# Recurrent stage of a hybrid block: products with rows by direction, the second direction's time reversed, and full-row transpositions

## The chip, the cores and the metric

The kernel runs on one core of a Trainium2 chip. The metric is the device time of one execution in microseconds, as the median over runs. The core's engines are PE (matmul), DVE (VectorE), ACT (ScalarE), POOL (GpSimd) and SP (SyncE), each with its own program; they order each other by semaphores.

## The reference

Two transformer blocks on 512 tokens of 1024 features. The change lies in the second block's RWKV-7 mixer: four pairs of heads (head size 64), a forward and a backward scan over 256 context tokens (no output), then over 512 latent tokens from the state reached, and the two directions' outputs are summed. Cut to its core:

```python
def rwkv_scan(s0, r, decay, k, v, kk, a, reverse, emit):
    def step(s, inp):
        w_t, k_t, v_t, kk_t, a_t = inp[:5]
        s_kk = jnp.einsum('bhvk,bhk->bhv', s, kk_t)
        s = (s * w_t[:, :, None, :]
             - s_kk[..., None] * (kk_t * a_t)[:, :, None, :]
             + v_t[..., None] * k_t[:, :, None, :])
        y = jnp.einsum('bhvk,bhk->bhv', s, inp[5]) if emit else None
        return s, y
```

`decay` and `a` come, for each direction, from a low-rank product with its own bias (w0, w_lora_b, a0, a_lora_b); `kk` is the normalized key.

## The kernel before

The recurrent stage computes the scan in 12 chunks of 64 tokens, both directions in the same chunk: chunks 0 to 3 are the context (quiet: no output), chunks 4 to 11 the latent tokens (they emit). Everything is f32. A chunk has 16 matrices of 64x64: 4 head pairs (q) x 2 heads of a pair (h) x 2 directions (d). In SBUF a tile of 128 partitions x 64 columns holds the two heads of (q, d), one in each half of the partitions; eight such tiles (n = 4d + q) make an operand of 512 columns. A product is 16 matmuls of 64 rows, written by `tiles` (L2026, matmul at L2031): ALONG leaves a matrix on its half of the partitions, ACROSS changes halves. An operand with features on the partitions (kap, rho, kt, bt, state) is "feature-major", one with tokens there (AT, CT, R1, R2, vt, kT, bT, Gs, Us) "token-major".

For each chunk c:

- The decays, two chunks ahead. `lora_in_act` (L1918) makes the low-rank input (tanh, L1925), `lora_pe` (L2057) multiplies it: 16 matmuls with 64 rows and 128 stationary columns (L2068). DVE adds the bias (`logits`, L2285), ACT takes the sigmoid (L1934), DVE's scan sums over time (L2295, and L2297 with time reversed for direction 1), ACT exponentiates (L1941, L1942, L1944), and POOL and DVE multiply: kap (L1906), rho (L1909, emitting chunks), kt (L1914), bt (L2314).
- The pair products of chunk n = c+1, in banks of PSUM: AT = bt x kap, CT = kt x kap, R1 = kt x rho, R2 = bt x rho, and the transpositions kT, bT and vt as products with the identity. DVE masks CT, R1 and R2 out of PSUM (`masked`, L2334); ACT copies AT, kT, bT, vt (`pair_copy`, L1964). `pair_XT` and `pair_X` (L2330) prepare X = I + masked AT and its transpose.
- The inverse of the triangular matrix, in five levels l. `level_Y` (L2110): 16 matmuls of 32 columns; DVE's `level_y` multiplies them by the level's mask (L2345); `level_W` (L2121): 16 matmuls more; DVE's `level_x` adds (L2353) and transposes (L2357). Each of these is in two groups, by direction.
- The state products of chunk s = c-1: Gold = kap x state and Gnew = CT x vt into the same bank, copied by ACT (Gs); U = X^T x Gs, copied (Us); Z = kT x vt + bT x Us, added to the state by DVE (`state_add`, L2363) and decayed (`state_decay`, L2369); y, an old part rho x state and a new part R1 x vt + R2 x Us, copied by ACT for chunks 4 to 7 (`y_copy`, L1954) and added by DVE for chunks 8 to 11 (`y_sum`, L2376).

The order is written out by hand in the loops over c of `rwkv_pe`, `rwkv_dve`, `rwkv_act` and `rwkv_pool`. `beside` issues two products alternately, one tile of each in turn, `alone` one. Before, PE's order in a chunk is: Y1 beside Gold(s); Gnew(s); low-rank product of c+2; W1 beside vt(c); Y2; U(s); W2 beside AT(n); Y3 beside CT(n); W3 beside Z(s); Y4 beside kT(n); W4, first group, beside the old part of y(s); new part of y(s); W4, second group, beside bT(n); Y5 beside R1(n); W5 beside R2(n).

## Time and profile before

| | us |
|---|---|
| median of 3 runs | 3107.16 (3104.86 to 3117.13) |
| profiled execution | 3118.53 |
| its span | 3116.9 |
| recurrent stage, chunks 0 to 11 in the profiled execution | 2153.0 to 2448.3 |
| mean granted clock of TensorE, as a share of full speed | 0.950 |

Times in the trace are microseconds from the start of the span. A matmul in f32 leaves two records on PE and two weight loads on PEld, a transposition one of each. PEclk is the clock that was granted, as a share of the full 2.4 GHz. In a wait, "issue" means that the engine waited for nothing that the profile shows. A chunk is cut here where the first matmul of its level 1 starts.

### The profile page before, as it was taken

Reading aid. Unit: us, or ns where it says so; the run is one execution under the profiler, and the core shown is the slowest. Engines: PE = TensorE matmul, PEld = TensorE weight load, DVE = VectorE, ACT = ScalarE, POOL = GpSimd, SP = SyncE. Lnnn points to the kernel's source line nnn. Section 1 sums busy time; section 2 is a strip of 40 time slices with the busy share of each in tenths; the row PEclk is TensorE's granted clock in tenths of the full one; section 3 lists DMA queues with packets and bytes.
Section 4 is the critical chain, followed back from the end, with each engine's and each line's share of the span. In section 5 each row is a group of like instructions: output and inputs, shape, how many; then the busy total and the mean of one; then the engine's idle time right before and its main releaser. Section 6 shows DMA issues by size and latency. Waiting matters only on the chain. (4 is left out here: it accounts for less than half of the span.)

```text
span 3116.9 us, 53002 instructions
## 1 busy us (share of the span) xinstructions
PE 2816.6 (90%) x20916; PEld 2297.6 (74%) x20916; DVE 1773.3 (57%) x2734; ACT 1417.7 (45%) x1913; POOL 850.6 (27%) x515
## 2 busy tenths in 40 slices
PE   9999999998989899999997999997877688799996
PEld 7887877776768687788774787776777465688884
DVE  3115456788999642311445402446776554699996
ACT  4445545555663232444344222334433222588884
POOL 3444451220004343344432234222332131000001
PEclk9999999999999999999998999997998788899997
DMA  3225371112222132222552122221000023899996
GB/s 125 94 95 188 135 280 64 42 61 66 80 81 98 61 122 88 88 94 95 187 189 85 54 75 85 75 78 52 5 4 4 29 81 115 326 412 411 412 411 243
DMA packets 110379, 412.30 MB, mean 132 GB/s; under 512 B 12064, under 2 KB 12080, under 8 KB 109312
## 3 DMA queue, kind: packets, MB, share of 16 engines
q1 hardware_dynamic: 88560, 322.24, 28.4%
q0 software_dynamic: 11136, 48.26, 4.2%
q10 hardware_dynamic: 10512, 39.33, 3.5%
q8 instruction: 131, 2.15, 0.3%
q14 instruction: 40, 0.33, 0.0%
HBM read 370.45 MB, written 39.32 MB: 131 GB/s over the span
## 5 line engine op out<-in xcount | busy, mean ns | idle before, releaser
L219 POOL TENSOR_TENSOR ring_r<-ring,whi 128x1024 fp32r<-128x1024 f32 x241 | 591.3, 2463 | 1017.4 <-ACT whi L214 1008.0
L231 PE MATMUL psum<-xn_r,whi 128*128 128x512 f32 x1176 | 460.1, 391 | 0.0
L214 ACT ACTIVATE whi<-ring 128x1024 fp32r<-128x1024 f32 x247 | 256.0, 1054 | 421.1 <-DMA ring<-stream 420.8
L229 PE MATMUL psum<-xh,ring_r 128*128 128x512 f32 x936 | 388.6, 415 | 28.1 <-DVE ring_r L219 20.5
L2813 DVE TENSOR_TENSOR er_r<-er,eh 128x1024 fp32r<-128x1024 f32 x268 | 309.5, 1219 | 1.0 <-ACT eh L2802 0.4
L2802 ACT ACTIVATE eh<-er 128x1024 fp32r<-128x1024 f32 x268 | 268.2, 1072 | 40.3 <-DMA er<-experts 39.6
L2031 PE MATMUL psum<-mem 64*64 64x64 f32 (+1 forms) x7744 | 214.8, 231 | 69.8 <-issue 24.8
L229 PE MATMUL psum<-ffn_xh,ring_r 128*128 128x512 f32 x672 | 261.4, 389 | 0.0
L230 PE MATMUL psum<-ffn_xh,whi 128*128 128x512 f32 x672 | 261.4, 389 | 0.0
L2031 PEld LDWEIGHTS psum<-mem 64*64 64x64 f32 x7744 | 200.8, 145 | 81.2 <-issue 55.1
L231 PEld LDWEIGHTS psum<-xn_r,whi 128*128 128x128 f32 x1176 | 222.1, 189 | 47.3
L229 PEld LDWEIGHTS psum<-xh,ring_r 128*128 128x128 f32 x936 | 178.4, 191 | 85.4 <-DVE ring_r L219 24.1
L563 DVE TENSOR_TENSOR gu<-gu,psum 128x512 f32<-128x512 f32 x44 | 30.3, 688 | 335.0 <-ACT gu L538 335.0
L230 PE MATMUL psum<-xh,whi 128*128 128x512 f32 x504 | 198.8, 394 | 0.0
L467 DVE TENSOR_TENSOR mem<-mem 128x1024 f32<-128x1024 f32 x64 | 127.9, 2026 | 76.3 <-ACT mem L449 71.6
L231 PE MATMUL psum<-xn_r,whi_h 128*128 128x512 f32 x432 | 170.2, 394 | 0.0
L230 PE MATMUL psum<-xh,whi_h 128*128 128x512 f32 x432 | 170.2, 394 | 0.0
L229 PE MATMUL psum<-hid_hi,ring_r 128*128 (+1 forms) x352 | 144.6, 411 | 13.1 <-POOL ring_r L219 13.1
L2873 PE MATMUL psum<-er_r,xbh 128*128 128x512 f32 x368 | 146.7, 399 | 3.4 <-DVE er_r L2813 2.0
L229 PEld LDWEIGHTS psum<-ffn_xh,ring_r 128*128 128x128 f32 x672 | 126.1, 188 | 26.3
L230 PEld LDWEIGHTS psum<-ffn_xh,whi 128*128 128x128 f32 x672 | 126.1, 188 | 26.1
L2875 PE MATMUL psum<-eh,xbl 128*128 128x512 f32 x368 | 144.5, 393 | 0.0
(527 smaller groups left out, 6031.3 us busy)
## 6 DMA issues: line engine op xcount, KB each, us to landing
ring<-stream SPq DMA_DIRECT2D x311, 512.0 KB, 3.3
er<-experts SPq DMA_DIRECT2D x276, 512.0 KB, 8.2
mem<-mod_w ACTq DMA_DIRECT2D x48, 512.0 KB, 3.5
xs_dram<-zero_row POOLq DMA_DIRECT2D x1, 12288.0 KB, 41.6
xs<-xs_dram SPq DMA_DIRECT2D x23, 512.0 KB, 8.1
ys_dram<-y_t ACTq DMA_DIRECT2D x23, 512.0 KB, 6.7
spill<-resid POOLq DMA_DIRECT2D x2, 2048.0 KB, 26.6
resid<-spill POOLq DMA_DIRECT2D x2, 2048.0 KB, 9.9
```

What stands on the lines that cost most here:

```text
L214: act.activation(high_of(part, j), w, ACT.Copy).then_inc(w_hi, 1)
L219: pool.tensor_tensor(ring_r[:, s, :, :], ring[:, s, :, :], f(high_of(part, j)), ALU.subtract).then_inc(w_lo, 1)
L229: pe.matmul(bank, lo[:, b, :], x_hi_, start=start, stop=False, skip_group_check=True)
L230: pe.matmul(bank, hi[:, b, :], x_hi_, start=False, stop=False, skip_group_check=True)
L231: return pe.matmul(bank, hi[:, b, :], x_lo_, start=False, stop=stop, skip_group_check=True)
L467: dve.tensor_tensor(mod_t[at % 2], mod_wb[m % 4], mod_c[:, s, :], ALU.mult).then_inc(mod_mul, 1)
L563: dve.tensor_tensor(gu[:, half, :], gu[:, half, :], psum[:, 2 * half, :], ALU.mult).then_inc(sg_ready, 1)
L2031: ins = pe.matmul(psum[o, bank, first:first + wide], lhs(n)[r], rhs(n)[r], start=i == 0 if start is None else start, stop=i == len(terms) ...
L2802: act.activation(eh[:, SLOT[kind] + j, :], er[:, SLOT[kind] + j, :], ACT.Copy).then_inc(e_hi, 1)
L2813: dve.tensor_tensor(er_r[:, at, :], er[:, at, :], f(eh[:, at, :]), ALU.subtract).then_inc(e_lo_dve, 1)
L2873: pe.matmul(bank, x_hi_, lo_[:, cols], start=start, stop=False, skip_group_check=True)
L2875: return pe.matmul(bank, x_lo_, hi_[:, cols], start=False, stop=stop, skip_group_check=True)
```

## The change

- Rows go by direction. Token-major operands hold direction 0 on partitions 0 to 63 and direction 1 on 64 to 127, so the two groups of a level are now the heads of a pair (h), not the directions. The second direction is stored with its time reversed from the start (`seq` and rho's product read it with a step of -1), so one mask serves both directions (576 columns fewer are transferred) and DVE's scan runs one way.
- kap and rho lie side by side, and `joint` multiplies one stationary tile of bt by both: AT and R2 come from one product, 16 matmuls with 128 moving columns (64 in quiet chunks). Likewise CT and R1 from kt.
- kT, bT and vt are 12 full transpositions of 128x128 in a chunk (`turned`, L2104), no longer 48 matmuls of 64x64. For vt POOL first copies v into `vs` (two copies a chunk).
- The low-rank product is 8 matmuls of 128 rows over a block-diagonal input (`lwd`, filled by four activations in place of two), not 16 of 64.
- Gnew lies beside Y1 and Gold is alone; the state and y products go to other quadrants and banks (6 and 7).
- PE's order in a chunk is: Y1 beside Gnew(s); Gold(s); low-rank product of c+2; W1; Y2; U(s); W2 beside AT+R2(n); Y3; W3 beside Z(s); Y4; kT(n); bT(n); W4, first group, beside the old part of y(s); new part of y(s); W4, second group; Y5; W5 beside CT+R1(n); vT(n).
- ACT's copy of vt stands at the end of the chunk, before the second half of the decays of c+2 and the low-rank inputs of c+3.

The operands:

```diff
-        kap, rho = [take(W8, "b") for _ in range(3)], [take(W8, "b") for _ in range(3)]
-        bt, kt = take(W8, "b"), take(W8, "b")
+        turn = lambda v, d: v.rearrange("p (q d t) -> p q d t", q=4, d=2)[:, :, d, :]
+        KR = [take(2 * W8, "b") for _ in range(3)]
+        kap, rho = [v[:, 0:W8] for v in KR], [v[:, W8:2 * W8] for v in KR]
+        bt, kt, vs = take(W8, "b"), take(W8, "b"), take(W8, "b")
...
-        lw_c = take(2 * L, "b")
+        lwd = take(4 * L, "b").rearrange("p (m t) -> p m t", m=2)
...
-        M_BANK = dict(vt=6, AT=4, CT=6, kT=4, bT=5, R1=6, R2=4)
+        TURNED_BANK = dict(kT=2, bT=3, vt=2)
...
+            pool.memset(lwd, 0.0).then_inc(filled, 1)
...
+                    pool.tensor_tensor(turn(kap[c % 3], d), seq(None, c, d), half(pexc, d), ALU.mult).then_inc(pool_p.sem, 1)
...
-                        pool.tensor_tensor(half(rho[c % 3], d), seq(0, c, d), half(pinc, d), ALU.mult).then_inc(pool_p.sem, 1)
+                        o = first_token(c, d)
+                        decay = half(pinc, d)[:, :, ::-1] if d else half(pinc, d)
+                        pool.tensor_tensor(turn(rho[c % 3], d), Z[:, 0:4, o:o + L], decay, ALU.mult).then_inc(pool_p.sem, 1)
...
-                        pool.wait_ge(pe_m.sem, pe_m.at(c - 1, "R1" if emits(c - 1) else "kT"))
-                    pool.tensor_tensor(half(kt, d), half(tk, d), half(pinv, d), ALU.mult).then_inc(pool_p.sem, 1)
+                        pool.wait_ge(pe_m.sem, pe_m.at(c - 1, "CT"))
+                    pool.tensor_tensor(turn(kt, d), half(tk, d), half(pinv, d), ALU.mult).then_inc(pool_p.sem, 1)
+                for d in range(2):
+                    if c and d == 0:
+                        pool.wait_ge(pe_m.sem, pe_m.at(c - 1, "vt"))
+                    pool.tensor_copy(turn(vs, d), seq(8, c, d)).then_inc(pool_p.sem, 1)
...
+            else:
+                act.wait_ge(filled, FILLS["lora"])
+            for m, f_ in ((0, ACT.Tanh), (1, ACT.Copy)):
+                for d in range(2):
+                    o = first_token(c, d)
+                    rows = slice(64 * d, 64 * d + 64)
+                    src = Z[rows, 12 + m, o:o + L]
+                    ins = act.activation(lwd[rows, m, d * L:(d + 1) * L], src[:, ::-1] if d else src, f_)
             ins.then_inc(act_w.sem, 1)
...
+                act.wait_ge(pe_m.sem, pe_m.at(c, "AT"))
+                act.activation(AT[c % 2].rearrange("p (b t) -> p b t", b=2), psum[:, 4:6, 0:4 * L], ACT.Copy).then_inc(act_m.sem, 1)
 
```

PE's products:

```diff
+            crossed = [(q, h, h ^ w) for q in range(4) for w in (1, 0) for h in range(2)]
+            level = [(q, h, d) for h in range(2) for q in range(4) for d in range(2)]
+            LOW, HIGH = slice(0, 8), slice(8, 16)
...
                 W(act_w, c, "lw")
-                for d in range(2):
-                    if c:
-                        W(dve_p, c - 1, f"t{d}")
+                if c:
+                    W(act_m, max(c - 2, 0), "vt")
                 for m in range(2):
                     for q in range(4):
-                        for d in range(2):
-                            o = first_token(c, d)
-                            r = ROWS[d]
-                            src = lw_c[r, 0:L] if m == 0 else Z[r, 13, o:o + L]
-                            ins = pe.matmul(psum[:, 2 + d, (4 * m + q) * L:(4 * m + q + 1) * L], wlo[m][r, q * P:(q + 1) * P], src,
-                                            start=True, stop=True)
-                            if m == 1 and q == 3:
-                                ins.then_inc(pe_w.sem, 1)
...
+            def joint(c, lhs):
+
+                def tile(q, h, d):
+                    w = 2 if emits(c) else 1
+                    out = psum[ROWS[d], 4 + h, :].rearrange("p (w q t) -> p w q t", w=2, q=4)[:, 0:w, q, :]
+                    moving = KR[c % 3].rearrange("p (w n t) -> p w n t", w=2, n=8)[ROWS[h], 0:w, 2 * q + d, :]
+                    return one(out, feat(lhs, q, d)[ROWS[h]], moving)
+                return tile
 
             def pair_AT(c):
                 for d in range(2):
                     W(dve_p, c, f"bt{d}")
-                W(pool_p, c, "kap1")
...
                 if c:
-                    W(dve_m, c - 1, "R2") if emits(c - 1) else W(act_m, c - 1, "kT")
-                return lambda n: tiles(n, M_BANK["AT"], (ACROSS, of(bt), of(kap[c % 3])))
+                    W(dve_m, c - 1, "R1" if emits(c - 1) else "CT")
+                return joint(c, bt)
 
...
             def pair_CT(c):
                 W(pool_p, c, "kt1")
-                if c:
...
-            def pair_R2(c):
+                W(act_m, c, "AT")
+                W(dve_m, c, "R2" if emits(c) else "XT")
+                return joint(c, kt)
...
+            def turned(bank, v):
+                for q in range(4):
+                    ins = pe.transpose(psum[:, bank, q * P:(q + 1) * P], v[:, q * P:(q + 1) * P], ident[:, :])
+                ins.then_inc(pe_m.sem, 1)
+
+            def turned_k(c):
+                W(pool_p, c, "kt1")
+                W(dve_p, min(c + 1, NCH - 1) if c else 0, "t1")
+                turned(TURNED_BANK["kT"], kt)
+
+            def turned_b(c):
+                turned(TURNED_BANK["bT"], bt)
+
+            def turned_v(c):
+                W(pool_p, c, "vs1")
...
-                return lambda n: tiles(n, M_BANK["R2"], (ACROSS, of(bt), of(rho[c % 3])))
-
-            def pair_vt(c):
...
+            def y_tile(q, h, d):
+                return psum[ROWS[1 - h], 6 + d, q * L:(q + 1) * L]
...
+                return lambda q, h, d: one(y_tile(q, h, d), feat(rho[c % 3], q, d)[ROWS[h]], state(st[c % 2], q, d)[ROWS[h]],
+                                           start=q == 0, stop=False)
...
                 W(pe_s, c, "ys")
-                return lambda n: tiles(n, 7, (ALONG, of(R1[c % 2]), of(vt[c % 2])), (ALONG, of(R2[c % 2]), of(Us)), start=False)
-
-            def level_Ys(c, l, other=None, done=None):
-                for d in range(2):
-                    y = level_Y(c, l, d)
+
+                def tile(q, h, d):
+                    one(y_tile(q, h, d), toks(R1[c % 2], q, h)[ROWS[d]], turned_toks(vt[c % 2], q, h)[ROWS[d]], start=False, stop=False)
+                    return one(y_tile(q, h, d), toks(R2[c % 2], q, h)[ROWS[d]], toks(Us, q, h)[ROWS[d]], start=False)
+                return tile
```

PE's order:

```diff
             pe.wait_ge(filled, FILLS["reset"])
             pe.wait_ge(kn_dve.sem, kn_dve.end(1))
-            alone(pair_AT(0), ALL, pe_m)
-            alone(pair_CT(0), ALL, pe_m)
+            alone(pair_AT(0), crossed, pe_m)
+            turned_k(0)
+            turned_b(0)
+            alone(pair_CT(0), crossed, pe_m)
+            turned_v(0)
             lora_pe(1)
-            alone(pair_kT(0), ALL, pe_m)
-            alone(pair_bT(0), ALL, pe_m)
             for c in range(NCH):
                 n, s = c + 1, c - 1
-                more, last, y, r = n < NCH, c > 0, emits(s), n < NCH and emits(n)
+                more, last, y = n < NCH, c > 0, emits(s)
                 if last:
-                    level_Ys(c, 1, state_G_old(s), pe_s)
...
                 else:
                     level_Ys(c, 1)
                 if c + 2 < NCH:
                     lora_pe(c + 2)
-                v = pair_vt(c)
...
+                    alone(level_W(c, 1, g), level[part], pe_l)
                 level_Ys(c, 2)
                 if last:
-                    alone(state_U(s), ALL, pe_s)
-                w = level_W(c, 2, 0)
+                    alone(state_U(s), level, pe_s)
+                a = pair_AT(n) if more else None
+                for g, part in enumerate((LOW, HIGH)):
+                    w = level_W(c, 2, g)
+                    if more:
+                        beside(w, level[part], pe_l, a, crossed[part], pe_m if g else None)
+                    else:
+                        alone(w, level[part], pe_l)
+                level_Ys(c, 3)
+                z = state_Z(s) if last else None
+                for g, part in enumerate((LOW, HIGH)):
+                    w = level_W(c, 3, g)
+                    if last:
...
-                    beside(w, LOW, pe_l, z, HIGH, pe_s)
-                else:
-                    alone(w, LOW, pe_l)
-                    alone(level_W(c, 3, 1), LOW, pe_l)
...
                 else:
-                    alone(w, LOW, pe_l)
-                w = level_W(c, 4, 1)
+                    alone(w, level[LOW], pe_l)
+                alone(level_W(c, 4, 1), level[HIGH], pe_l)
+                level_Ys(c, 5)
+                k = pair_CT(n) if more else None
+                for g, part in enumerate((LOW, HIGH)):
+                    w = level_W(c, 5, g)
+                    if more:
...
-                else:
-                    level_Ys(c, 5)
-                if r:
-                    other = pair_R2(n)
-                    w = level_W(c, 5, 0)
-                    beside(w, LOW, pe_l, other, LOW)
-                    w = level_W(c, 5, 1)
-                    beside(w, LOW, pe_l, other, HIGH, pe_m)
-                else:
-                    alone(level_W(c, 5, 0), LOW, pe_l)
-                    alone(level_W(c, 5, 1), LOW, pe_l)
+                    turned_v(n)
```

Three places in the engines' orders. **PE, level 4 of chunk 8** (psum<-mem 64x32 are level matmuls, shared,mem 64x64 those of kT). Before:

```order
L2031 MATMUL psum<-mem 64x32 [waits rwkv_dve_levels,rwkv_dve_pairs]
L2031 MATMUL psum<-mem 64x32
L2031 MATMUL psum<-shared,mem 64x64 x2
L2031 MATMUL psum<-mem 64x32 x2
L2031 MATMUL psum<-shared,mem 64x64 x2
L2031 MATMUL psum<-mem 64x32 x2
...
L2031 MATMUL psum<-mem 64x32 x2
L2031 MATMUL psum<-shared,mem 64x64 x2
L2031 MATMUL psum<-mem 64x32 [waits rwkv_dve_state,rwkv_dve_levels]
L2031 MATMUL psum<-mem 64x32
```

and now:

```order
L2053 MATMUL psum<-mem 64x32 [waits rwkv_dve_levels]
L2053 MATMUL psum<-mem 64x32 x7
L2053 MATMUL psum<-mem 64x32 [waits rwkv_dve_levels]
L2053 MATMUL psum<-mem 64x32 x7
L2104 MATMUL psum<-ident,mem 128x128 [waits rwkv_dve_decay,rwkv_pool_decay]
L2104 MATMUL psum<-ident,mem 128x128 x7
L2053 MATMUL psum<-mem 64x32 [waits rwkv_dve_state,rwkv_dve_levels]
L2053 MATMUL psum<-mem 64x64
```

Y4's sixteen matmuls stand alone, and eight transpositions (L2104) that wait for the decays of DVE and POOL stand between them and W4.

**DVE, levels 4 and 5 of the same chunk** (L2334, now L2348, are the masks of CT, R1 and R2; L2345 the level's multiplication, L2353 its sum, L2363 the state's sum, L2376 the sums of y). Before:

```order
L2363 TENSOR_TENSOR mem<-mem,psum 128x512 [waits rwkv_pe_state]
L2334 TENSOR_TENSOR mem<-psum,shared 128x512 [waits rwkv_pe_pairs]
L2302 SCALAR_TENSOR_TENSOR mem<-zero_row,pv 128x256 [waits rwkv_pool_decay]
L2353 TENSOR_TENSOR mem<-mem,psum 128x8x16 [waits rwkv_dve_levels,rwkv_pe_levels] x2
L2357 STREAM_TRANSPOSE mem<-mem 128x256 [waits rwkv_dve_levels] x2
L2369 TENSOR_TENSOR mem<-mem 128x512 [waits rwkv_dve_decay,rwkv_dve_state]
L2295 SCALAR_TENSOR_TENSOR resid<-mem,zero_row 128x256 [waits rwkv_pool_decay,rwkv_act_decay]
L2345 TENSOR_TENSOR mem<-psum,shared 128x4x32 [waits rwkv_pe_levels] x2
L2302 SCALAR_TENSOR_TENSOR mem<-zero_row,pv 128x256 [waits rwkv_pool_decay]
L2334 TENSOR_TENSOR mem<-psum,shared 128x512 [waits rwkv_pe_pairs]
L2353 TENSOR_TENSOR mem<-mem,psum 128x4x32 [waits rwkv_dve_levels,rwkv_pe_levels] x2
L2334 TENSOR_TENSOR mem<-psum,shared 128x512 [waits rwkv_pe_pairs]
```

and now (L2359 the level's multiplication, L2366 its sum, L2377 the state's sum, L2390 the sums of y):

```order
L2377 TENSOR_TENSOR mem<-mem,psum 128x512 [waits rwkv_pe_state]
L2319 SCALAR_TENSOR_TENSOR mem<-zero_row,pv 128x256 [waits rwkv_pool_decay]
L2366 TENSOR_TENSOR mem<-mem,psum 128x8x16 [waits rwkv_dve_levels,rwkv_pe_levels] x2
L2370 STREAM_TRANSPOSE mem<-mem 128x256 [waits rwkv_dve_levels] x2
L2383 TENSOR_TENSOR mem<-mem 128x512 [waits rwkv_dve_decay,rwkv_dve_state]
L2348 TENSOR_TENSOR mem<-psum,shared 128x512 [waits rwkv_pe_pairs,rwkv_pe_state]
L2313 SCALAR_TENSOR_TENSOR resid<-mem,zero_row 128x256 [waits rwkv_pool_decay,rwkv_act_decay]
L2359 TENSOR_TENSOR mem<-psum,shared 128x4x32 [waits rwkv_pe_levels] x2
L2319 SCALAR_TENSOR_TENSOR mem<-zero_row,pv 128x256 [waits rwkv_pool_decay]
L2366 TENSOR_TENSOR mem<-mem,psum 128x4x32 [waits rwkv_dve_levels,rwkv_pe_levels] x2
L2348 TENSOR_TENSOR mem<-psum,shared 128x512 [waits rwkv_pe_pairs] x2
L2390 TENSOR_TENSOR mem<-mem,psum 128x256 [waits rwkv_act_state,rwkv_pe_state]
```

The mask of R2 moves from behind level 5's sum to before its multiplication, those of CT and R1 behind its sum.

**ACT, the end of a chunk.** Before:

```order
L1964 ACTIVATE mem<-psum 128x512 [waits rwkv_pe_pairs] x2
L1941 ACTIVATE resid<-resid 128x256 [waits rwkv_pool_decay,rwkv_dve_decay]
L1942 ACTIVATE mem<-resid 128x256
L1944 ACTIVATE mem<-std 128x256 [waits rwkv_pool_decay]
L1925 ACTIVATE mem<-mem 64x64 [waits rwkv_pe_lora]
L1925 ACTIVATE mem<-mem 64x64
```

and now (L1981 copies kT, bT and vt, L1954 to L1957 are the decays, L1938 the low-rank inputs):

```order
L1981 ACTIVATE mem<-psum 128x512 [waits rwkv_pe_pairs] x3
L1954 ACTIVATE resid<-resid 128x256 [waits rwkv_pool_decay,rwkv_dve_decay]
L1955 ACTIVATE mem<-resid 128x256
L1957 ACTIVATE mem<-std 128x256 [waits rwkv_pool_decay]
L1938 ACTIVATE mem<-mem 64x64 [waits rwkv_pe_lora]
L1938 ACTIVATE mem<-mem 64x64 x3
```

The copy of vt is third of three, ahead of the decays, and the low-rank inputs are four.

## Rows read from the trace of the kernel before

**Rows 1.** The page: each engine's busy time and instructions; a group of this stage's line.

```profile
PE 2816.6 (90%) x20916; PEld 2297.6 (74%) x20916; DVE 1773.3 (57%) x2734; ACT 1417.7 (45%) x1913; POOL 850.6 (27%) x515
...
L2031 PE MATMUL psum<-mem 64*64 64x64 f32 (+1 forms) x7744 | 214.8, 231 | 69.8 <-issue 24.8
```

**Rows 2.** Windows (busy us of PE, PEld, DVE, ACT, POOL; PEclk): chunks 0, 1, 1-4, 8, 9.

```profile
2153.00:2179.60 26.60, 19.36 (x525) 18.73 (x520) 19.12 (x48) 13.59 (x30) 10.94 (x13) 0.62 0.01 3
2179.60:2200.10 20.50, 16.70 (x672) 15.55 (x672) 15.70 (x46) 9.23 (x19) 6.46 (x9) 1.00 0.02 4
2179.60:2267.80 88.20, 69.76 (x2816) 65.59 (x2817) 66.23 (x189) 37.18 (x77) 28.80 (x38) 0.96 0.02 4
...
2346.60:2372.70 26.10, 19.55 (x836) 18.25 (x837) 16.64 (x48) 9.81 (x21) 8.39 (x12) 1.00 0.02 4
2372.70:2401.00 28.30, 23.81 (x842) 22.52 (x832) 18.69 (x52) 8.75 (x17) 8.07 (x11) 0.82 0.02 4
```

**Rows 3.** Windows, chunks 0 to 11; then DMA, instruction queue, same stretch and 1950 to 2100.

```profile
2153.00:2448.30 295.30, 230.29 (x8910) 217.33 (x8905) 197.34 (x554) 104.67 (x217) 82.20 (x104) 0.91 0.02 4
...
q8 instruction: 70, 1.15, 1.7%
...
q8 instruction: 6, 0.10, 0.3%
```

**Rows 4.** Waits of PE from 2153 to 2458: total us, times, longest.

```profile
PE psum L2031 <- issue: 28.6, 29, 1.7
PE psum L2031 <- DVE mem L2363: 8.9, 7, 1.6
...
PE psum L2031 <- DVE mem L2376: 4.6, 3, 2.0
```

**Rows 5.** Chain of waits in chunk 8: shares by line, and one piece.

```profile
by line: PE psum L2031 59.3%; issue 21.1%; PE psum L2068 7.4%; DVE mem L2357 5.2%; DVE mem L2345 2.4%; DVE mem L2363 2.3%; DVE mem L2353 2.2%; DVE mem L2330 0.4%; DVEq L2276 0.1%
...
2370.78 1.58 issue
```

**Rows 6.** Timeline of PE: start, us, line, stationary rows x columns, moving, xcount.

```profile
2346.61 1.04 PE L2031 MATMUL psum<-mem 64*64 64x32 f32 x55 [0.83 <-DVE mem L2353]
...
2348.60 1.15 PE L2031 MATMUL psum<-mem 64*64 64x64 f32 x32
...
2349.68 2.00 PE L2068 MATMUL psum<-mem,shared 64*128 64x64 f32 x32
...
2352.65 0.77 PE L2031 MATMUL psum<-mem 64*64 64x32 f32 x19
...
1961.27 0.82 PE L1655 MATMUL psum<-ident,resid 128*128 128x128 f32 x6
...
2124.50 0.70 PE L2184 MATMUL psum<-mem,shared 128*128 128x512 f32 x1
...
2124.50 1.12 PE L2184 MATMUL psum<-mem,shared 128*128 128x512 f32 x2
```

**Rows 7.** Groups by line, 2145 to 2460: busy us, mean ns; then ACT's timeline.

```profile
L2334 DVE TENSOR_TENSOR mem<-psum,shared 128x512 f32<-128x512 f32 x28 | 19.0, 679 | 1.3 <-PE psum L2031 1.3
...
L1964 ACT ACTIVATE mem<-psum 128x512 f32<-128x512 f32 x48 | 28.5, 594 | 86.7 <-PE psum L2031 86.7
...
L1914 POOL TENSOR_TENSOR mem<-mem 128x256 f32<-128x256 f32 x24 | 20.3, 847 | 14.1 <-DVE mem L2307 14.1
...
2121.91 0.51 ACT L1925 ACTIVATE mem<-mem 64x64 f32<-64x64 f32 x2
```

**Rows 8.** Windows and timeline of PE where the clock is at half.

```profile
2155.80:2176.30 20.50, 15.78 (x397) 0.50 0.01 3
2374.30:2384.50 10.20, 10.20 (x188) 0.50 0.01 3
...
2374.13 1.88 PE L2031 MATMUL psum<-mem 64*64 64x64 f32 x32 [0.17 <-PE psum L2031]
...
2663.68 1.94 PE L2860 MATMUL psum<-ident,xs 128*128 128x128 f32 x8 [20.76 <-DMA xs<-xs_dram]
```

322 lines of the change are left out of this document (149 added, 173 removed).

## The prediction

> **What bounds the kernel now.** The page first: PE is busy for 90% of the span, DVE for 57% [rows 1]. The change touches only the recurrent stage, so I read the rest there. The windows by chunk show twelve chunks of 20 to 28 us each, with PE busy for three quarters, and chunk 0 and part of chunk 9 at a lowered clock [rows 2]. The two are chained: each level of the inverse goes PE, DVE, PE, DVE, and the other products are packed beside it.
>
> A second limit shows in the DMA view. The queue for instructions moves 70 packets, 1.15 MB, in 295.3 us of this stage, and PE and its weight loads have 17815 records there: 64.5 bytes each, some 254 records to a packet. Where the matmuls are 512 columns wide the same queue moves 6 packets in 150 us [rows 3]. So this stage, and only this one, eats a packet every 4.2 us. PE's waits fit: the largest is "issue", no semaphore at all, 28.6 us in 29 times, at most 1.7 each; DVE's state add stands for 8.9 us, the y sums for 4.6 [rows 4]. In the chain of chunk 8 "issue" has 21.1%, with a piece of 1.58 us among products whose operands are ready [rows 5]. I read: PE runs out of instructions about once in every 10 us.
>
> **Prices.** A matmul here is two records. A record shows some 0.2 us of its own (231 ns in the mean [rows 1]) but overlaps the next, so I take 0.2 off a group's time. 32 records of 64x64 alone take 1.15 us, so 30 ns each; 19 of 32 columns take 0.77, 30 ns too, so the width is not paid below 64. Both use two of the four quadrants: a quadrant needs 60 ns per record. 55 records of a level product beside a state product take 1.04 us over four quadrants, which agrees. The low-rank product: 32 records in 2.00 us, 56 ns. Full transpositions: 6 in 0.82 us, 0.10 to 0.11 each. A 512-column record follows its neighbour by 1.12-0.70=0.42 us (one alone, and two), so 128 columns are 0.107 [rows 6]. A DVE mask is 0.68 us; ACT's copy 0.59, its two low-rank inputs 0.51; a POOL product 0.85 [rows 7].
>
> **The change, part by part**, against the profiled execution of 3118.5 us (11.4 above the median of 3107.2).
>
> *Instructions.* An emitting chunk goes from 832 to 668 PE records, a quiet one from 672 to 572 (each with its weight load): 9280 to 7568 over the stage, and 70 packets to 57. The stalls named "issue" are 28.6 us. Bounds: all gone, -28.6; shrinking only with the packets, -5. An emitting chunk will need 5.3 packets (668 records and as many weight loads) in some 25 us, one in 4.7 us where its 832 need 6.5 in 26 now, one in 4.0, so I take three quarters: **-21.5**.
>
> *Emitting chunks 5 to 10*, each:
> - Gnew now lies beside level 1 on the same two quadrants (64 records x 30 ns = 1.92 where it was 0.96), Gold alone on four (0.48, where Gnew alone was 0.96): +0.48.
> - AT and R2 in one tile of 128 columns beside W2. Per half the level's quadrants have 8 records at 0.06 and 4 wide ones at 0.107, 0.91 where it was 0.48: +0.87. If a wide tile costs what a narrow one does it is +0.48.
> - CT and R1 likewise beside W5, which R2 shared before: +0.87.
> - The new part of y on four quadrants instead of two: 32 x 0.06 = 1.92 to 0.96: -0.96.
> - bT no longer lies beside the second half of W4: -0.48. CT, kT and R1 leave level products that stay as long without them: 0.
> - kT and bT by full transpositions, 8 x 0.11 = 0.88, stand before W4. They lie under DVE's transposition of X, the level's masks and the state add, for which PE waits up to 1.6 us a chunk now [rows 4]; nothing. Without that cover, +0.9. The transpositions of v follow the last level product, under DVE's level-5 add, 0.44; +0.2 is left.
> - DVE masks R2 before the level-5 product instead of after: Y5 is done, and W5 waits for it: +0.68. CT's and R1's masks come after level 5's adds, where the next chunk's level 1 does not need them.
> - ACT now copies vt before the second half of the decays and makes four low-rank inputs: 0.6 more wait, and 0.5 more work, before the low-rank product. That product is 16 x 0.107=1.7 where it was 2.0: together +0.2.
>
> Sum +1.86, times 6: **+11.2**. The extra POOL copies (two of 0.85 at most) and ACT's lie on engines that are busy for 8 to 10 of 26 us [rows 2]: nothing, unless v's copies come after kt late enough to hold PE's last product.
>
> *Quiet chunks 1 and 2*: the narrow forms give +0.48+0.48+0.48-0.48+0.2+0.2=1.36 each. *Chunks 3 and 4* add the wide tiles (2 x 0.39) and R2's mask: 2.82 each. Together **+8.4**. *Chunk 0* has no Gold; it runs at half clock, where 32 records alone need 1.88 us, not 1.15, and a transposition 0.22 [rows 8]: **+2.5**. *Chunk 11 and the tail*: y's new part twice -0.96, Gold +0.48 once and -0.48 once: **-1.9**. *Chunks 10 and 11* start with a state product that waits for the y sums; those now stand behind two masks instead of one: 2 x 0.68 = **+1.4**.
> *Before the stage*: two more low-rank inputs and a POOL memset, against products on four quadrants: 0. *The masks' transfer* (576 columns fewer) is long done when it is needed: 0.
>
> Against the change of array shape speaks a rule. In the rows, the low-rank product starts 1.08 us after its 32 neighbours of 64x64 did, that is 0.07 before the last of them ends [rows 6]: a change of shape costs at most that record's 0.2 us. Shapes change six times a chunk now instead of twice. I count 0.2 of it, as v's transpositions, since the others fall where PE waits anyway. The Trainium skill (TensorEngine Tiling (Array Packing), Key Properties) says that changing the tiling mode, not only the tile, drains TensorE. By that rule, as an estimate with the 0.2 of the row, three more of the four new ones would cost: 12 x 0.6 = 7 us, 3114. No row here shows a shape change that costs more than the last record's time.
>
> Sum: -21.5+11.2+8.4+2.5-1.9+1.4 = +0.1. Profiled 3118.6, as a median **3107**.
>
> **Rivals.**
> *A: the supply alone decides.* The chunk's time follows its records, and PE's packing only fills what the supply leaves. For it: 672 records take 20.5 us, 836 take 26.1, 842 take 28.3 [rows 2], 31 to 34 ns each whatever their mix. Against it: 55 records in 1.04 us [rows 6] are 19 ns each, so between stalls PE is ahead of the supply's mean, and the chain shows DVE's links as well. Price: 13 packets x 4.2 = -55, 3052; if half the added products show, about 3075. Nothing here shows how the queue prefetches. The Trainium skill (Advanced Engine Details and Errata, ISA Cache) gives cache lines of 16 KB, 256 instructions, and only two of them; the packets of rows 3 agree in size.
>
> *B: slower, by the clock.* Place: the quiet chunks. The granted clock is at its lower level (0.50, 1.2 GHz) in 2155.8 to 2176.3 although PE is busy for 15.8 of 20.5 us, and again for 10 us in chunk 9 [rows 8]; it rose only at the end of chunk 0. The change takes products out from beside the level products (levels 3 and 5 stand alone) and makes 12 of a chunk's products transpositions. If the clock stays down through chunk 4, 572 records at chunk 0's 50.7 ns (26.6 us over 525) are 29.0 us each, 116 for four, where I forecast 96.6: +19.5, 3127. It decides from three such chunks on; one or two stay within the bound of a measurement. Against: over chunks 1 to 4 the clock is 0.96 now [rows 2]. The Trainium skill (TensorE: Matmul & The Clock Gate, Part 4: PE-mode transpose) says that transposes do not count as PE activity in the same way. By that, chunk 9's 10 us at half clock would come more often. No row of this stage holds a transposition, so the trace cannot tell.
>
> *C: nothing of it shows.* The stalls move to other places and the additions are hidden: 3107 as well, for another reason.
>
> **How the numbers follow.** My forecast has 0.55; with its bounds (supply -28.6 to -5, wide tiles 0.48 or 0.87, cover of kT and bT gone) it reaches from 3092 to 3128. A has 0.22, B 0.18, C 0.05. Half a per cent, 15.5 us, is about what a measurement can tell from no change: 3091.6 to 3122.7. Of the forecast 0.12 falls below and 0.08 above; A is all faster; of B 0.16 is slower and 0.02 inside; C is inside. So faster 0.34, same 0.42, slower 0.24. The range 3072 to 3132 leaves out the further half of A (0.11) and some 0.07 at the top.
>
> **What would show it.** Right: 57 or 58 packets of instructions from chunk 0 to 11; "issue" before PE under 10 us; an emitting chunk of 24.5 to 26 us at full clock, a quiet one of 21 to 24; W2 and W5 with their joint tiles 1.8 us instead of 0.96; a wait for DVE's mask multiply before W5 longer by 0.7; no wait for ACT's vt copy or POOL's v copy before v's transpositions; y's new part about 1 us. A is right if emitting chunks take 21 us. B is right if the clock by chunk is under 0.8 in chunks 1 to 4. The forecast is wrong if "issue" stays above 20 us (then about 3120), or if a wide tile turns out to cost what a narrow one does (6 us less), or if W4 starts later by the transpositions of k and b.

## The result, and the profile after

| | before | changed |
|---|---|---|
| median | 3106.9 us (4 runs) | 3162.2 us (3156.1 to 3169.4, 4 runs) |
| ratio | 1 | 1.0161, 95% interval [1.0139, 1.0182] |
| profiled execution's span | 3116.9 us | 3161.9 us |
| stage, from chunk 0's level 1 to the last product | 2153.0 to 2456.7: 303.7 us | 2153.4 to 2502.9: 349.5 us |
| of it at half clock (from the trace's clock records) | 54.6 us in 8 stretches | 158.4 us in 11 stretches |
| after the stage | 660.2 us | 659.0 us |

The change is 1.6% slower, 55.3 us in the medians. In the profiled executions the spans differ by 45.0 us, since that of before was 11.4 above its median, and all of it lies in the recurrent stage: 45.8 us more there, 0.4 more up to its start, 1.2 less behind it. The page of the changed kernel, which answers to [rows 1]:

```profile
span 3161.9 us, 49630 instructions
...
PE 2882.1 (91%) x19204; PEld 2357.9 (75%) x19204; DVE 1782.9 (56%) x2734; ACT 1421.8 (45%) x1937; POOL 861.5 (27%) x540
```

PE has 1712 matmul records fewer and is busy 65.5 us longer. The windows say why. Chunks 0, 1, 1 to 4, 5, 8 and 9 of the changed kernel (columns as in [rows 2]: length, busy time of PE, PEld, DVE, ACT, POOL, granted clock):

```profile
2153.40:2186.00 32.60, 25.65 (x413) 24.21 (x412) 20.73 (x50) 11.71 (x25) 11.85 (x15) 0.55 0.01 2
2186.00:2211.90 25.90, 24.15 (x575) 22.69 (x574) 15.98 (x46) 9.44 (x21) 7.23 (x10) 0.76 0.01 3
2186.00:2287.20 101.20, 90.99 (x2291) 85.46 (x2290) 66.84 (x187) 37.76 (x84) 32.09 (x44) 0.84 0.01 3
2287.20:2312.70 25.50, 22.39 (x669) 20.73 (x668) 18.74 (x50) 10.10 (x23) 9.06 (x12) 0.95 0.01 3
2373.90:2404.10 30.20, 26.88 (x671) 25.18 (x670) 17.24 (x49) 10.10 (x23) 8.58 (x12) 0.78 0.01 3
2404.10:2436.20 32.10, 27.48 (x671) 25.52 (x670) 18.41 (x51) 10.85 (x25) 8.59 (x12) 0.77 0.01 3
```

Chunk 5, at 0.95, takes 25.5 us: what the prediction gave an emitting chunk at full clock (24.5 to 26). Chunk 8, with the same work (671 records, 669 in chunk 5), takes 30.2 us at 0.78. In windows of PE alone, one cycle of it (length, PE busy, granted clock):

```profile
2382.10:2399.10 17.00, 14.14 (x491) 1.00 0.01 3
2399.10:2412.80 13.70, 13.24 (x182) 0.50 0.01 3
```

491 records in 17.0 us at 2.4 GHz, then 182 in 13.7 at 1.2 GHz. Chunk by chunk, in us, with the time at half clock behind the stroke:

| chunk | 0 | 1 | 2 | 3 | 4 | 5 | 6 | 7 | 8 | 9 | 10 | 11 and tail |
|---|---|---|---|---|---|---|---|---|---|---|---|---|
| before | 26.6/20.5 | 20.5/0 | 22.8/3.4 | 21.5/0 | 23.4/3.4 | 26.0/3.4 | 25.5/0 | 27.3/3.4 | 26.0/0 | 28.4/10.2 | 25.3/4.3 | 30.3/6.0 |
| changed | 32.6/29.2 | 25.8/12.2 | 25.8/8.7 | 25.4/7.9 | 24.1/3.4 | 25.6/2.3 | 31.3/14.3 | 29.8/12.7 | 30.2/13.2 | 32.1/15.0 | 31.0/17.4 | 35.7/22.0 |

Before, the clock fell 8 times and, outside chunks 0 and 9 and the last one, for 3.4 us each. Now it falls once in every chunk but chunk 3, in all but one of them for 10 to 17 us (37.5 in chunk 0); a stretch that begins at the end of a chunk is counted mostly in the next. Where it falls is seen in PE's timeline at the end of chunk 8 (start, us, line, form, count, wait ahead):

```profile
2394.80 2.54 PE L2053 MATMUL psum<-mem 64*64 64x64 f32 x107
2399.41 0.94 PE L2053 MATMUL psum<-mem 64*64 64x32 f32 x16 [2.07 <-DVE mem L2359]
```

PE stands for 2.07 us before W5, waiting for DVE's multiply by the mask of level 5; the clock falls at 2399.1, inside that wait. The same holds for the others: of the ten falls behind chunk 0, nine come in such a wait of PE for L2359 or at most 1.3 us behind it (the waits are 1.4 to 2.1 us, and 0.6 behind a stall of 1.4 in chunk 9), and the last in a wait for the sums of y. What the low clock then costs is seen at the start of chunk 8 (low) and of chunk 5 (full), the same work:

```profile
2373.85 5.01 PE L2053 MATMUL psum<-mem 64*64 64x32 f32 x96
2378.79 3.60 PE L2053 MATMUL psum<-mem,shared 128*128 128x128 f32 x16
...
2287.15 2.13 PE L2053 MATMUL psum<-mem 64*64 64x32 f32 x64
2289.44 0.69 PE L2053 MATMUL psum<-mem 64*64 64x64 f32 x32 [0.15 <-PE psum L2053]
2290.06 2.05 PE L2053 MATMUL psum<-mem,shared 128*128 128x128 f32 x16
```

Y1 beside Gnew, Gold and the low-rank product take 8.5 us in chunk 8 and 5.0 in chunk 5, and the clock rises only as they end, at 2382.1. PE's waits of the changed kernel, 2153 to 2503 (us, times, longest), which answer to [rows 4]:

```profile
PE psum L2053 <- DVE mem L2359: 20.5, 22, 2.1
PE psum L2053 <- ACT mem L1938: 6.6, 1, 6.6
PE psum L2053 <- issue: 6.4, 6, 1.6
PE psum L2053 <- DVE mem L2390: 4.0, 3, 1.4
PE psum L2053 <- DVE mem L2377: 4.0, 6, 1.1
```

and the instruction queue over chunks 0 to 11 in the DMA view, which answers to [rows 3]:

```profile
q8 instruction: 56, 0.92, 1.1%
```

"Issue" went from 28.6 to 6.4 us, as forecast, with 56 packets for 70. But the wait for the level's multiply (L2359) is 20.5 us. Before (L2345, from 2153 to 2458) it was

```profile
PE psum L2031 <- DVE mem L2345: 8.1, 13, 1.1
```

so PE's waits have moved to one place in the chunk.

### The profile page after: what moved, and what is told of

Same layout as the page of the kernel before. It is cut to its first block and busy times, and to the rows that moved or that the text cites. A ratio compares the mean times of both kernels' runs of the same rounds, so it can differ in the third digit from the quotient of the medians.

```text
span 3161.9 us, 49630 instructions
## 1 busy us (share of the span) xinstructions
PE 2882.1 (91%) x19204; PEld 2357.9 (75%) x19204; DVE 1782.9 (56%) x2734; ACT 1421.8 (45%) x1937; POOL 861.5 (27%) x540
## 3 DMA queue, kind: packets, MB, share of 16 engines
q8 instruction: 117, 1.92, 0.2%
## 5 line engine op out<-in xcount | busy, mean ns | idle before, releaser
L2053 PE MATMUL psum<-mem 64*64 64x32 f32 (+2 forms) x7232 | 252.5, 252 | 51.9 <-DVE mem L2359 20.5
L2053 PEld LDWEIGHTS psum<-mem 64*64 64x64 f32 x7232 | 238.5, 159 | 67.1 <-issue 54.5
L563 DVE TENSOR_TENSOR gu<-gu,psum 128x512 f32<-128x512 f32 x44 | 30.3, 688 | 336.3 <-ACT gu L538 336.3
## 6 DMA issues: line engine op xcount, KB each, us to landing
spill<-resid POOLq DMA_DIRECT2D x2, 2048.0 KB, 26.6
```

Of the source, the lines that this page charges most:

```text
L2053: return pe.matmul(out, lhs, rhs, start=start, stop=stop, skip_group_check=True)
```

## The experiments

Every ratio is against runs of the kernel before on the same chip. Half clock: us of the stage, from the clock records of the profiled execution. That is one execution of several, and not always a typical one: that of e5 took 3123.1 us at a mean clock of 0.949, where three of its other four ran at 0.943 to 0.944, and that of e9 took 3155.2 us at 0.938, where the other three ran at 0.942 to 0.944.

| run | median, us | ratio [95%] | stage, us | at half clock |
|---|---|---|---|---|
| changed | 3162.2 | 1.0161 [1.0139, 1.0182] | 349.5 | 158.4 |
| e1_hold | 3121.6 | 1.0031 [1.0012, 1.0050] | 306.4 | 50.3 |
| e2_mult | 3145.1 | 1.0101 [1.0081, 1.0121] | 330.9 | 83.4 |
| e3_scan | 3138.2 | 1.0089 [1.0066, 1.0113] | 320.1 | 101.7 |
| e4_gold | 3143.6 | 1.0112 [1.0081, 1.0143] | 326.1 | 102.4 |
| e5_before_lull | 3131.5 | 1.0067 [1.0041, 1.0093] | 313.8 | 68.3 |
| e6_twice | 3141.4 | 1.0110 [1.0086, 1.0135] | 327.9 | 81.9 |
| e7_best | 3108.3 | 1.0002 [0.9989, 1.0015] | 295.8 | 13.7 |
| e8_before_hold | 3104.8 | 0.9990 [0.9975, 1.0006] | 304.8 | 54.6 |
| e9_before_both | 3147.9 | 1.0131 [1.0109, 1.0153] | 345.9 | 139.9 |
| e10_many | 3142.3 | 1.0119 [1.0098, 1.0140] | 330.5 | 78.1 |
| e11_order | 3133.2 | 1.0104 [1.0072, 1.0136] | 322.3 | 109.2 |
| e12_best | 3108.3 | 1.0012 [0.9998, 1.0027] | 295.5 | 13.7 |

**e1_hold: fill the gap before W5.**

```diff
+            def hold(n, times):
+                W(act_m, n, "bT")
+                for i in range(times):
+                    pe.matmul(psum[:, 3, 0:P], ident[:, :], ident[:, :], start=True, stop=True, skip_group_check=True)
...
                 level_Ys(c, 5)
+                if more:
+                    hold(n, 9 if emits(n) else 6)
```

> The changed kernel with 9 (emitting next chunk) or 6 extra matmuls of 128x128 by 128 columns between level 5's Y products and W5, where PE waits 1.4 to 2.1 us for DVE's mask multiply; they write a bank that nobody reads then, 0.9 to 1.3 us of TensorE at each such place per 6, all inside the wait. Theory 'clock by the lull': the clock falls in every chunk because PE is nearly idle there; with the gap filled the clock stays at 1.0 from chunk 1 on, emitting chunks take 25 to 26 us where they took 30 to 32, and the kernel takes 3115 to 3130 instead of 3162. Rival 'clock by the transpositions': they are unchanged, the fall moves at most; within 10 us of 3162. Rival 'the added work is what costs': the clock does not matter, 3162 to 3170.

Measured 1.0031. Chunks 1 to 4 and chunk 8 in the windows:

```profile
2184.80:2271.00 86.20, 84.33 (x2354) 79.27 (x2354) 67.97 (x188) 37.79 (x85) 32.59 (x44) 1.00 0.02 4
2345.70:2370.30 24.60, 23.34 (x689) 21.99 (x688) 18.34 (x49) 10.10 (x23) 9.07 (x12) 1.00 0.02 4
```

No fall from chunk 1 to chunk 10. Twelve or eighteen records a chunk of work that nobody uses take chunks 1 to 4 from 101.2 to 86.2 us and chunk 8 from 30.2 to 24.6, where the kernel before needed 88.2 and 26.1 [rows 2]. That is 1.3% of the kernel, four fifths of the loss, as the theory of the lull had it (3115 to 3130). So the clock is what costs, and work in the lull before W5 keeps it up. That the place matters, and not only the added work, this run alone does not show; the next two add work elsewhere.

**e2_mult: the transpositions as plain matmuls; e6_twice: each transposition twice.**

```diff
-                    ins = pe.transpose(psum[:, bank, q * P:(q + 1) * P], v[:, q * P:(q + 1) * P], ident[:, :])
+                    ins = one(psum[:, bank, q * P:(q + 1) * P], v[:, q * P:(q + 1) * P], ident[:, :])
```

> The changed kernel with its 12 transpositions a chunk done as plain f32 matmuls by the same 128x128 identity: 12 records a chunk more, 12 x 0.107 = 1.3 us of TensorE. Theory 'transpositions do not count for the clock': the clock falls less often (mean over chunks 0 to 11 above 0.88 where it is 0.78) and the kernel comes to 3120 to 3145. Theory 'clock by the lull': the lull before W5 stays, the mean clock stays within 0.04 of 0.78 and the time lies at 3160 to 3175, since the extra 1.3 us per chunk fall partly under waits.

Measured 1.0101, and the mean clock of the stage rose from 0.77 to 0.87 (0.89 over chunks 0 to 11). That is what I had written for the transpositions, and it is against the theory of the lull as I had written it, clock and time: by this run alone the transpositions would look guilty. But it also adds 12 records a chunk. e6 adds the same number as transpositions:

```diff
                 for q in range(4):
+                    for i in range(2):
-                    ins = pe.transpose(psum[:, bank, q * P:(q + 1) * P], v[:, q * P:(q + 1) * P], ident[:, :])
+                        ins = pe.transpose(psum[:, bank, q * P:(q + 1) * P], v[:, q * P:(q + 1) * P], ident[:, :])
```

> The changed kernel with each of the 12 transpositions a chunk made twice: 12 records a chunk more, the same number as with plain matmuls by the identity (which gave a ratio of 1.0101 and 83 us at half clock where the changed kernel has 158). Theory 'transpositions do not count for the clock': no help, half clock 150 us or more, ratio 1.016 to 1.020. Rival 'any work on TensorE counts, and the plain matmuls only filled time': 80 to 110 us at half clock and a ratio of 1.009 to 1.013.

Measured 1.0110 and 81.9 us at half clock, against 1.0101 and 83.4: any work counts, as the rival had it. The stage of e2 in the windows:

```profile
2153.20:2484.20 331.00, 288.97 (x7594) 273.15 (x7592) 205.04 (x557) 109.47 (x238) 93.46 (x126) 0.87 0.01 3
```

and that of e6:

```profile
2153.70:2481.60 327.90, 286.43 (x7593) 269.41 (x7592) 205.79 (x557) 109.43 (x238) 93.63 (x126) 0.88 0.01 3
```

Twelve more transpositions a chunk did as much for the clock as twelve more records of plain matmuls of the same size; what helped in both was more work. The suspicion of the transpositions falls. Both runs also say that work away from W5 helps: it halves the time at half clock and takes back about a third of the loss, where e1's work before W5 takes back four fifths (with 12 records for a quiet next chunk, 18 for an emitting one). Twelve or eighteen records at another place, to the same number as in e1, were not run.

**e3_scan: a shorter lull.**

```diff
-                if next_too:
-                    cumulate(c + 2, 1)
                 level_y(c, 5)
                 if next_too:
+                    cumulate(c + 2, 1)
                     key_mix(c + 2, 1)
```

> The changed kernel with DVE's scan of c+2 behind level 5's mask multiply instead of ahead of it: the wait before W5 shrinks by 0.68 us (2.1 to 1.4 in emitting chunks, 1.4 to 0.7 in quiet ones). Theory 'clock by the lull': quiet chunks, where 0.7 is left, keep the clock, emitting ones may not; 12 x 0.7 = 8 us for the wait alone and 10 to 25 us more by the clock: 3130 to 3152. Rival 'clock by the transpositions' or 'by work on two quadrants': only the wait goes: 3150 to 3158, mean clock as it was, 0.78.

1.0089: 0.7% back, 22 us, of which the wait itself can be 8. Half clock went from 158 to 102 us, with no work added. By chunk: 3, 7, 8 and 9 kept the clock, 4 and 6 for all but their last 3 us, 1, 2, 5 and 10 did not. It is in the range of the lull theory, though not split by quiet and emitting as I had said.

**e4_gold: the opening of the chunk on four quadrants.**

```diff
-                    level_Ys(c, 1, state_G_new(s), level, pe_s)
-                    alone(state_G_old(s), crossed, pe_s)
+                    level_Ys(c, 1, state_G_old(s), crossed, pe_s)
+                    alone(state_G_new(s), level, pe_s)
```

(The waits and the start of the accumulation change places with them, in the tail too.)

> The changed kernel with Gold beside level 1 again and Gnew alone (as before the change): the same records, but the first 4 us of a chunk use four quadrants first. Theory 'work on two quadrants does not raise the clock': the stretch at half clock, 13.7 us a chunk now and until after the low-rank product, ends before that product, 5 to 7 us earlier; at half the speed that gives back 2 to 3 us a chunk, 3130 to 3145. Theory 'the lull alone': falls and rises stay, 3155 to 3165.

1.0112. The clock still falls 11 times, but six of the stretches last 3.4 us, where the changed kernel has one of that length; 1.0112 is what I had written for work on two quadrants (3130 to 3145). So two things bear on the clock: the lull on whether it falls, and the opening on how long it stays low.

**e5_before_lull and e9_before_both: the same, in the kernel before.** e5 adds two scans on DVE ahead of level 5's multiply, which makes PE's wait for that multiply as long as in the changed kernel (19.9 us in the stage, at most 2.3, for 8.1 and 1.1 before):

```diff
+                if d and c >= 2:
+                    for i in range(2):
+                        dve.tensor_tensor_scan(idle[:, i, :], reset, sw, 0.0, ALU.mult, ALU.add)
```

> The kernel before, with two more DVE scans (0.68 us each, into a spare tile) ahead of the scan that precedes level 5's mask multiply, in chunks 0 to 9; nothing else. So W5 waits up to 1.4 us longer, 10 times. By the wait alone: at most +14, ratio up to 1.0045. Theory 'a lull before W5 drops the clock': the clock falls in most chunks, the share of the stage at half clock grows from 55 us of 304 to 90 or more, and the kernel is 20 to 40 us slower. Rival 'what makes the clock fall are the transpositions and the bare level products': this kernel has neither, the clock stays as it was, +5 to +14.

1.0067, 21 us where the wait alone can give 14. In the trace the falls go from 8 to 11, but most last 3.4 us and the half clock is 68 us of 314, short of the 90 that I had written. The three executions at 0.943 to 0.944 must have had more: 0.005 to 0.006 of 3130 us are, as an estimate, 31 to 38 us more at half clock, some 100 to 106. The lull alone costs 0.67% here, wait and clock together, where the change cost 1.61. e9 adds to e5 the opening of the changed kernel:

```diff
-                    level_Ys(c, 1, state_G_old(s), pe_s)
-                    alone(state_G_new(s), ALL, pe_s)
+                    level_Ys(c, 1, state_G_new(s), pe_s)
+                    alone(state_G_old(s), ALL, pe_s)
```

> The kernel before with both suspects of the changed one: the two extra DVE scans ahead of level 5's multiply (with these alone: 11 falls of the clock, 68 us of 314 at half clock, ratio 1.0067), and Gnew beside level 1, Gold alone, so that each chunk opens with 64 records on two quadrants. Theory 'the lull makes the clock fall, two-quadrant work keeps it down': still about 11 falls, but each lasts 7 to 14 us instead of 3.4; 95 to 140 us at half clock, ratio 1.011 to 1.018. Rival 'only the lull, and transpositions or bare levels keep it down': 60 to 80 us at half clock, ratio 1.006 to 1.009.

1.0131, as forecast, and 139.9 us at half clock in 14 stretches, nine of them of 10 us or more. The stage of before in the windows:

```profile
2153.00:2456.70 303.70, 236.91 (x9100) 223.36 (x9094) 197.34 (x554) 107.15 (x220) 82.20 (x104) 0.91 0.02 4
```

of e5:

```profile
2148.00:2461.80 313.80, 243.22 (x9098) 228.83 (x9094) 208.84 (x574) 107.13 (x220) 82.32 (x104) 0.89 0.02 4
```

and of e9:

```profile
2148.60:2494.50 345.90, 280.73 (x9097) 266.07 (x9090) 208.99 (x574) 106.95 (x220) 82.42 (x104) 0.80 0.01 4
```

With the same records as before, no transposition and no joint product, e9 falls into the swing of the changed kernel (0.80 against 0.77) by a longer wait at one place and the exchange of two products at another. The step from e5 to e9 is shown by the medians, 0.6% or 20 us with intervals apart. The traces overstate it: by the clocks of all executions (medians 0.944 and 0.9425) the two differ, as an estimate, by some 10 us at half clock and not by 72. Of the 20 us the half clock would then explain 5, and the opening's own work, at 0.48 us a chunk by the prediction's prices, another 5; the rest is open. The exchange alone was not run on this kernel, so what it does without the lull stays open too.

**e10_many: is "issue" the supply of instructions?** As e1, with 30 pairs (20 in quiet chunks) of small matmuls:

```diff
+                for i in range(times):
+                    for h in range(2):
+                        pe.matmul(psum[ROWS[h], 3, 0:32], ident[ROWS[h], ROWS[h]], ident[ROWS[h], 0:32], start=True, stop=True, skip_group_check=True)
```

> The changed kernel with the gap before W5 filled by many small matmuls: 60 of 64x64 by 32 columns before an emitting chunk (40 before a quiet one), on two quadrants and so 120 records of 15 to 30 ns, where e1_hold had 9 of 128x128 by 128 columns (18 records). A chunk then has 788 records instead of 668, near the 832 of before. Theory 'PE runs out of instructions': waits named issue come back, 15 to 30 us where e1_hold has under 5, whatever the clock does; ratio at least 1.006. Rival 'issue gaps were something else of the old order': under 8 us, and the ratio is that of e1_hold, 1.003, or 1.016 if two-quadrant work does not hold the clock.

Waits of PE in e10, 2151 to 2446:

```profile
PE psum L2053 <- ACT mem L1938: 6.6, 1, 6.6
...
PE psum L2053 <- issue: 1.2, 2, 0.8
```

The waits did not come back: 1.2 us with 8661 records in 330.5 us. As I had put it, the theory falls: the number of instructions in a chunk does not decide. What the records show is narrower. In the kernel before, between chunks 1 and 11, 25 weight loads start more than 0.6 us behind their predecessor without a semaphore; each of them starts 1.26 to 1.59 us after the end of an instruction packet's transfer. Two of the "issue" pieces in its chain of waits, chunk 8:

```profile
2367.32 0.99 issue
...
2370.78 1.58 issue
```

and its DMA view from 2366.0 to 2374.0 (40 slices of 0.2 us; a packet at 2369.4, one at 2373.6):

```profile
GB/s 0 0 0 0 0 0 0 0 0 0 0 0 0 0 0 0 0 82 0 0 0 0 0 0 0 0 0 0 0 0 0 0 0 0 0 0 0 0 82 0
```

The second piece ends at 2372.36, 2.8 us after the packet of 2369.55 begins, the first at 2368.31, 2.6 after that of 2365.71. So the stalls are waits for packets. Which packets come late stays open. It is not those that follow each other closely: at the 25 stalls the packet begins 3.4 to 4.8 us behind the one before it, and between chunks 1 and 11 before has 26 of 60 such distances under 3.8 us, e10 23 of 58, with two stalls. (The least distance is 3.4 us in before and 3.3 in e10; in the mean it is 4.0 in before, 4.4 in e10, 4.6 in e1.) e10's extra instructions lie in the gap, where PE had time anyway. Its ratio of 1.0119 is not from "issue". The clock falls four times, for 41 us from chunk 0 on (which took 36.4 us), for 17 us in chunks 7 and 8, and twice at the end; and the added matmuls are more work than e1's: chunks 2 to 6, at full clock in both, take 120.7 us where e1 has 115.6. That small matmuls on two quadrants hold the clock less surely than e1's fits this one trace, and is not shown beyond it.

**e7_best, e12_best, e8_before_hold, e11_order: what can be had.** e7 is e3 with `hold` before W5 (6 or 4), in chunk 0 (6 of 512 columns in the wait for the low-rank input, 4 before W3 and W4) and in chunk 11 and the tail.

```diff
                 else:
                     level_Ys(c, 1)
+                    hold(7, 6, 4 * P)
```

> The changed kernel with DVE's scan behind level 5's multiply, and extra matmuls that keep the clock: before W5 in every chunk (6 or 4), in chunk 0 during the wait for the low-rank input (6 of 512 columns, 5.2 us) and before W3 and W4, and in chunk 11 and the tail. If the clock is the whole loss, and the extra matmuls stay inside waits: no fall from chunk 1 on, chunk 0 at 24 us instead of 33, the scan's 0.7 us a chunk saved: 3095 to 3110 where before is 3115 on this kind of run, ratio 0.992 to 0.998. If the extra matmuls delay the level products: ratio 1.000 to 1.005.

1.0002: the kernel before is reached, not passed by the 0.2 to 0.8% that I had hoped for. The stage took 295.8 us, at 0.98:

```profile
2152.10:2447.80 295.70, 272.68 (x7639) 252.83 (x7638) 202.67 (x556) 108.36 (x238) 93.81 (x126) 0.98 0.01 4
```

The stage is 7.9 us shorter than in the profiled execution of before, and the medians are equal. That execution was 11.4 above its own median, and the runs of before spread from 3096.9 to 3119.6 with granted clocks of 0.949 to 0.958, the shorter ones at the higher clock: an average run of before has probably a shorter stage than the profiled one, which no trace shows. Some is lost ahead of the stage, where POOL's fills stand in a row and ACT's inputs wait for the last one:

```profile
2120.01 0.54 POOL L1881 MEMSET mem<- 128x512 f32 x1
2120.47 0.33 POOL L1882 MEMSET mem<- 128x256 f32 x1
2120.86 0.40 POOL L1884 MEMSET mem<- 128x4 f32 x1
2120.90 0.80 POOL L1885 MEMSET mem<- 128x512 f32 x1
2121.64 0.72 POOL L1886 MEMSET mem<- 128x256 f32 x1
...
2123.58 0.77 PE L2053 MATMUL psum<-mem,shared 128*128 128x128 f32 x2 [4.59 <-ACT mem L1938]
```

The first low-rank matmul starts 5.2 us after the transpositions that precede it (2118.39); in the kernel before it was 1.8. e12 puts the fill (L1886) first.

```diff
+            pool.memset(lwd, 0.0).then_inc(filled, 1)
             pool.memset(st[0], 0.0).then_inc(filled, 1)
...
-            pool.memset(lwd, 0.0).then_inc(filled, 1)
```

> e7_best with the memset of the low-rank input first of POOL's fills. e7_best gave 1.0002 although its stage took 295.8 us against 303.7 of before; in its trace 4.9 us pass between the last matmul of the attention part and the first of the low-rank product, where before has 1.5. That product waits for ACT, and ACT for a memset that stands behind four others on POOL. With it first: 2 to 3 us less, ratio 0.9985 to 0.9995. If the wait is for something else, 1.0002 again.

1.0012 [0.9998, 1.0027]. In its trace PE stands for 2.94 us ahead of the first low-rank matmul, where e7 has 4.60; no gain shows in the median, since the expected 2 to 3 us lie within the spread of the runs (3096.3 to 3115.5).

> The kernel before with only the extra matmuls in chunk 0's wait for the low-rank input (6 of 512 columns). Theory 'clock': the 20.5 us at half clock in chunk 0 go or shrink to 7, 7 to 10 us saved, ratio 0.997 to 0.998. Rival: the clock falls later in chunk 0 anyway, since its levels have nothing beside them: ratio 0.999 to 1.001.

e8 is the same filling of chunk 0's wait, in the kernel before: 0.9990 [0.9975, 1.0006]. Chunk 0 took 22.1 us without any half clock, 4.5 less; other chunks of that execution lost it again (chunk 6 took 30.4 us, 13.7 of them low), 54.6 us at half clock as before. It was the longest of the ten, 10.8 us above their median. No difference in the medians, and not for the reason that I had given: chunk 0 kept its clock.

e11 joins e3, e4 and the earlier fill, with no useless work:

> The changed kernel with no extra work, in a better order: DVE's scan behind level 5's multiply, Gold beside level 1 and Gnew alone, and the memset of the low-rank input first of POOL's fills. Alone the first gave 1.0089 (102 us at half clock), the second 1.0112 (102 us). If the two act together (a shorter lull makes fewer falls, and each is shorter): 55 to 80 us at half clock, 3 us less before the stage, ratio 0.999 to 1.006. If they are the same gain twice: 1.008 to 1.010 less 0.001.

1.0104 [1.0072, 1.0136], 109.2 us at half clock: the two orders do not add up; together they gain no more than the first alone (1.0089). Its four runs go from 3127 to 3151. Without holding the clock by extra work no order that I tried reaches the kernel before.

## Why the prediction was wrong

**The result lies outside the range** (3162.2; forecast 3107, range 3072 to 3132), and slower had a chance of 0.24.

- *Supply.* "Issue" 28.6 us, forecast -21.5: 6.4 are left, -22.2. Right, and the coincidence with the packets holds: with the clock held (e1) a packet comes every 4.6 us, 4.7 forecast. The reason that I gave, the mean distance between packets, is not enough: e10 has 4.4 and 1.2 us of "issue".
- *Emitting chunks at full clock*, forecast 24.5 to 26: 25.5 in chunk 5, and 24.6 to 25.5 in chunks 5 to 8 of e1. Right. The quiet ones, 21 to 24: 25.4 to 25.8 in the changed kernel, 20.7 to 22.2 in e1. W5 with its joint tiles, 1.8 and the last record's 0.2 forecast, takes 2.04 in e1. The prices held: Y1 beside Gnew 2.13 (1.92 and the last record's 0.2), Gold 0.69 (0.48 and 0.2). The low-rank product, forecast 1.7, took 2.05: a record of 128 rows and 128 columns is 0.12, not 0.107, so nothing was gained there. The new part of y takes 1.2 us in the records of chunk 8 where it was 2.1; right too.
- *The wait for DVE before W5*, forecast 0.7 longer: it is 2.07 us in chunk 8, where before had none over 0.25. I counted only the mask of R2. The two chunks without that mask show that it is not all: in chunks 1 and 2 the wait is 1.36 and 1.47 us, for 1.11 and 1.12 before. R1's product had stood beside Y5 and bT's beside W4, and what they hid came out as well, as I read it; I had written 0 and -0.48 for them. In the sum over the stage the wait grew by 12.4 us (8.1 to 20.5), in which "issue" may have hidden some before. As time this is small. As a lull it is what the result hangs on.
- *Before the stage*, forecast 0: the first low-rank product starts 3.4 us later behind the transpositions, by POOL's fill; the stage itself starts only 0.4 later, since the transpositions came 2.4 earlier in this execution and 0.6 came back behind. Chunk 0, forecast +2.5: +6.0, with 29.2 us at half clock for 20.5.
- *The step that failed* is the clock. The sum was made at the clock of before, each term as work and waits, and nothing in it asked whether the edits would change the clock itself: a term put at nothing without a reason. Measured, the stage has 158.4 us at half clock for 54.6. The 103.8 us more are at most 51.9 us of time, and 45.8 were lost in the stage. Rival B did ask, with 0.18, but in the wrong place and at less than half the price: it kept the clock down through the quiet chunks (+19.5) and took as evidence against it that the clock of before is 0.96 there. The fall comes in nearly every chunk, emitting ones above all.
- *What the rest of the sum is worth* stays open to some 10 us. With the clock held (e1), chunks 1 to 10 take 238 us where before has 247, but before has 28 us at half clock there, up to 14 us of time. Over the whole stage e1 has about before's half clock (50.3 and 54.6 us) and takes 306.4 us for 303.7, with its added work. A gain of the change itself, the clock apart, is not shown.
- *The reasons of rival B.* "Levels 3 and 5 stand alone" pointed at the right spot. The part on transpositions was wrong: e6 and e2 give the same. The Trainium skill (TensorE: Matmul & The Clock Gate, Part 4: PE-mode transpose) says that they do not count as PE activity in the same way; here 12 more of them a chunk helped as much as 12 more records of plain matmuls (1.0110 and 1.0101), and the measurement decides.
- *The rule against the change of shape*. The Trainium skill (TensorEngine Tiling (Array Packing), Key Properties) says that a change of the tiling mode drains TensorE. It was not what cost: in chunk 5 the low-rank product begins 0.07 us before the last record of Gold ends (2290.06 against 2289.44 and 0.69), as before the change. The trace disagrees with a price above that.

What the trace of before could have told: of the seven falls of its clock after chunk 0, five come within 2 us of the turn of two chunks (2200.2, 2244.6, 2374.3, 2401.6, 2425.5). At each of them PE has just stood for 1.1 to 2.0 us, once for the multiply of level 5, three times in "issue", once for the sums of y; and in four of the five the clock is back 3.4 to 6.8 us later. The change took the "issue" away, made the wait for the multiply longer, and gave the two-quadrant product to the opening where the clock had come back.
